# First modulation pieces read by whole rows in 8 KB runs, summed over all four at once; load and compute order of the opening changed

## The reference, cut to what matters

```python
shift, scale, gate = jnp.split(jax.nn.silu(c) @ w_mod[l] + b_mod[l], 3, axis=-1)
shift_c, scale_c, gate_c = jnp.split(jax.nn.silu(c_ctx) @ w_mod[l] + b_mod[l], 3, axis=-1)
hc = rms_norm(xc, norm_w[l]) * (1.0 + scale_c) + shift_c
parts_c = split_in(hc @ w_in[l])
```

## Time and profile before

| | |
|---|---|
| median of 3 runs | 1619.99 us (1619.35 to 1620.15) |
| profiled execution, its own time | 1618.67 us |
| its span, first to last instruction | 1616.9 us |
| TensorE busy | 1520.1 us (94% of the span) |
| VectorE, ScalarE, GpSimd busy | 528.8, 454.2, 324.8 us |
| mean granted TensorE clock | 0.978 of full speed |
| moved by DMA | 233.82 MB, mean 145 GB/s |

### The profile page before, as it was taken

The page is one execution under the profiler, slowest core; times in us unless marked ns, Lnnn a source line. Parts: engine busy times, 40 slices in busy tenths (PEclk is TensorE's granted clock), DMA queues, the critical chain, the costliest instruction groups (busy, mean ns, idle before and its releaser), DMA issues.

```text
span 1616.9 us, 17425 instructions
## 1 busy us (share of the span) xinstructions
PE 1520.1 (94%) x6805; PEld 793.1 (49%) x6805; DVE 528.8 (33%) x1136; ACT 454.2 (28%) x890; POOL 324.8 (20%) x350
## 2 busy tenths in 40 slices
PE   5998989999999989999999999999999599989997
PEld 2676544455676454445675344455455433333332
DVE  1073310655533220565532211122143611212125
ACT  2234322232763232233762120133132110101112
POOL 1010000444000010456000000003522234323310
PEclk9999999999999999999999999999999789999999
DMA  9654114221120212111100131201500679999995
GB/s 348 240 212 179 53 54 154 79 105 52 32 77 1 94 52 77 54 53 52 53 3 1 52 104 62 94 2 52 177 36 14 265 264 401 372 415 391 409 419 231
DMA packets 85129, 233.82 MB, mean 145 GB/s; under 512 B 16824, under 2 KB 24766, under 8 KB 70840
## 3 DMA queue, kind: packets, MB, share of 16 engines
q1 hardware_dynamic: 70002, 204.03, 33.5%
q0 software_dynamic: 13824, 24.98, 4.2%
q10 hardware_dynamic: 1222, 3.70, 0.6%
HBM read 266.42 MB, written 16.80 MB: 175 GB/s over the span
## 4 chain that ended last, share of the span: by engine, by line
PE 89%; ACT 3%; DVE 3%; DMA 3%; issue 2%; POOL 0%; SPq 0%; DVEq 0%; POOLq 0%; ACTq 0%
PE PS L1779 19%; PE PS L2199 11%; PE PS L1947 9%; PE PS L2010 7%; PE PS L2225 5%; PE PS L1859 5%; PE PS L1758 4%; PE PS L2008 3%; PE PS L2103 3%; PE PS L1881 3%; PE PS L1869 3%; PE PS L1821 2%; PE PS L2045 1%; DMA RING<-in_w_mod_dram 1%; PE PS L2072 1%
## 5 line engine op out<-in xcount | busy, mean ns | idle before, releaser
L1779 PE MATMUL PS<-RH,RING 128*128 128x512 f32 (+1 forms) x864 | 315.9, 522 | 2.1 <-DMA RING<-in_w_in_dram 2.1
L1779 PEld LDWEIGHTS PS<-RH,RING 128*128 128x128 f32 x864 | 162.4, 190 | 146.9 <-issue 136.1
L1947 PE MATMUL PS<-RING,RY 128*128 128x512 f32 x320 | 139.4, 593 | 0.0
L2199 PE MATMUL PS<-RING,RM 128*64 128x512 f32 x384 | 116.6, 609 | 8.4 <-issue 5.6
L1277 DVE SCALAR_TENSOR_TENSOR RM<-RM,COL 128x512 f32<-128x512 f32 (+1 forms) x180 | 115.1, 707 | 0.2
L624 POOL TENSOR_SCALAR SMALL<-SMALL 128x1 f32<-128x1 f32 (+1 forms) x32 | 9.3, 290 | 525.8 <-ACT WS L852 266.0
L2010 PE MATMUL PS<-RH,RING 128*128 128x512 f32 x256 | 113.8, 593 | 0.0
L1318 DVE TENSOR_REDUCE SMALL<-PS 128x1 f32<-128x768 f32 (+1 forms) x80 | 68.0, 849 | 136.9 <-PE PS L1859 136.8
L1859 PE MATMUL PS<-RK,RH 96*128 96x256 f32 (+1 forms) x288 | 106.2, 488 | 1.1 <-ACT WS L995 0.7
L1947 PEld LDWEIGHTS PS<-RING,RY 128*128 128x128 f32 x320 | 60.1, 190 | 72.7 <-issue 72.7
L2199 PEld LDWEIGHTS PS<-RING,RM 128*64 128x64 f32 x384 | 37.1, 140 | 83.6 <-issue 80.1
(11 more groups left out here) (356 smaller groups left out, 2289.9 us busy)
## 6 DMA issues: line engine op xcount, KB each, us to landing
RING<-in_w_in_dram SPq DMA_DIRECT2D x18, 2048.0 KB, 8.5
RING<-in_w_mod_dram SPq DMA_DIRECT2D x12, 2048.0 KB, 9.0
RING<-in_w_expert_gate_dram SPq DMA_DIRECT2D x19, 1024.0 KB
RING<-in_w_expert_up_dram SPq DMA_DIRECT2D x19, 1024.0 KB
RING<-in_w_out_dram SPq DMA_DIRECT2D x8, 2048.0 KB, 8.8
RK<-in_w_expert_down_dram SPq DMA_DIRECT2D x8, 1024.0 KB
X<-in_w_expert_down_dram SPq DMA_DIRECT2D x8, 1024.0 KB
WS<-in_w_expert_down_dram SPq DMA_DIRECT2D x8, 1024.0 KB
```

Of the source, the lines that this page charges most:

```text
L1779: last = mm(o[:, 0:T], w[:, k, m * P:(m + 1) * P], HT[:, k, 0:T], start=(k == 0), stop=(k == 7))
L1947: last = mm(PS[:, j % 2, :], YT[:, k, t * P:(t + 1) * P], w[:, k, :], start=(k == 0), stop=(k == 7))
L2199: last = mm(PS[64 * z:64 * z + 64, n % 2, :], XGT[n % 2][:, k, 64 * z:64 * z + 64], free(GU[n % 3][z], [2048, 2], [1, DE], off=DE * k), st ...
```

## The change

The first four modulation pieces are no longer 512 columns of all rows, but 256 rows of the first 2048 columns each: a partition gets two runs of 8 KB in place of eight of 2 KB. TensorE adds all four pieces into one PSUM bank, column quarter z on partitions 32z to 32z+31 (8 matmuls per piece as before), ScalarE copies the bank once, four matmuls turn it into columns, and one VectorE addition and the two steps for `AMOD` (`scale_columns`) follow. The order changes on each engine: ScalarE squares the context rows before it copies the parameter columns; VectorE norms them first; TensorE waits for layer 0's parameter rows ahead of the third piece and transposes the context rows ahead of the fourth. SyncE issues pieces 4 and 5 (`in_low`, `in_feat` 2) ahead of the 16 small loads, and VectorE waits for the head weights only where it first uses them.

```diff
--- before.py
+++ after.py
@@ -420,9 +420,15 @@
         NW = len(plan)
         w_in_cols = {"in_low": (0, U0), "in_gate": (GA0, 512)}
 
+        def early(layer, n):
+
+            return layer == 0 and n < 4
+
         def chunk_view(key):
 
             kind, i, n = key
+            if kind == "mod" and early(i, n):
+                return RING[:, use[key] % 3, :].rearrange("p (k c) -> p k c", k=2)
             c = chunk_cols(key)[1]
             return RING[:, use[key] % 3, 0:8 * c].rearrange("p (k c) -> p k c", k=8)
 
@@ -454,6 +460,8 @@
         def chunk_source(key):
             kind, i, n = key
             c0, c = chunk_cols(key)
+            if kind == "mod" and early(i, n):
+                return a["w_mod"][0][2 * P * n:2 * P * n + 2 * P, 0:2048].rearrange("(k p) c -> p k c", p=P)
             if kind == "mod":
                 w = a["w_mod"][i]
             elif kind.startswith("in_"):
@@ -508,7 +516,7 @@
                 sp.dma_start(WUKV[:, :], a["w_ukv"][layer]).then_inc(s_lw, 16)
                 sp.dma_start(WPW[:, :, :], a["cf_pw_w"][layer].rearrange("(k p) c -> p k c", p=P)).then_inc(s_lw, 16)
 
-            for n in range(4):
+            for n in range(6):
                 load_chunk(n)
             for layer in range(2):
                 for m, name in enumerate(("q_head_norm_w", "k_head_norm_w")):
@@ -517,7 +525,7 @@
             sp.dma_start(OH, a["onehot"]).then_inc(s_oh, 16)
             sp.dma_start(RB[0:32, :], a["rel_bias_2"]).then_inc(s_oh, 16)
             load_rows(sp, R1, ROWS, s_rows[1], 1)
-            for n in range(4, NW):
+            for n in range(6, NW):
                 if plan[n] == ("mod", 0, 4):
                     load_layer_weights(0)
                 if plan[n] == ("in_feat", 0, 0):
@@ -1028,12 +1036,10 @@
                     act.wait_ge(p_gb.sem, p_gb.at(i, c))
                     A(GB[:, 512 * c:512 * c + 512], PS[:, 5 + c, :], ACT.Copy).then_inc(a_gb.sem, 1)
 
-            for n in range(4):
-                mod_rows(0, n, 6 + n % 2)
-                if n == 0:
-                    columns(0)
-                if n == 1:
-                    row_scale(0)
+            row_scale(0)
+            columns(0)
+            act.wait_ge(p_mr, 4)
+            A(MR_EARLY[0], PS[:, 6, :], ACT.Copy).then_inc(a_mr, 4)
             for i in (0, 1, 2, 3):
                 if i in (1, 2):
                     row_scale(i)
@@ -1182,6 +1188,11 @@
                 ins.then_inc(v_ch, 1)
                 v.wait_ge(v_ch, chain[0])
 
+            def scale_columns(layer):
+                link(v.tensor_scalar(AMOD[:, layer, :, :], MOD[:, layer, 8:16, :], 1.0, None, ALU.add))
+                nw = free(COL[:, layer, :], [1, 8], [0, 2], off=ROW["norm_w"])
+                return v.tensor_tensor(AMOD[:, layer, :, :], AMOD[:, layer, :, :], nw, ALU.mult)
+
             def modulation(layer, n, bank):
 
                 done = 6 * layer + n + 1
@@ -1192,9 +1203,7 @@
                 last = v.tensor_tensor(MOD[:, layer, c:c + 4, :], free(PS[:, bank, :], [2, 4], [1, 2]), bm, ALU.add)
                 if n == 3:
                     link(last)
-                    link(v.tensor_scalar(AMOD[:, layer, :, :], MOD[:, layer, 8:16, :], 1.0, None, ALU.add))
-                    nw = free(COL[:, layer, :], [1, 8], [0, 2], off=ROW["norm_w"])
-                    last = v.tensor_tensor(AMOD[:, layer, :, :], AMOD[:, layer, :, :], nw, ALU.mult)
+                    last = scale_columns(layer)
                 last.then_inc(v_mod, 1)
                 v.wait_ge(v_mod, done)
 
@@ -1213,8 +1222,6 @@
             def projections(i):
                 T = nt[i] * P
                 q = Q_RANK if i in FULL else 0
-                if i == 0:
-                    v.wait_ge(s_hw, 16 * 5)
                 for t in range(nt[i]):
                     v.wait_ge(g_ur.sem, g_ur.at(i, t))
                     if q:
@@ -1234,6 +1241,8 @@
                                else CFP[:, c - 10, 15:15 + T])
                         v.tensor_tensor(dst, dst, TMP[:, tmp % 2, 0:T], ALU.mult).then_inc(v_f.sem, 1)
                         tmp += 1
+                    if i == 0 and step_beside(i, j) == 0:
+                        v.wait_ge(s_hw, 16 * 5)
                     if step_beside(i, j) is not None and step_beside(i, j) < units[i]:
                         head_sums(i, step_beside(i, j))
                         head_scale(i, step_beside(i, j))
@@ -1384,10 +1393,13 @@
             v.tensor_reduce(PICK2[:, :], free(IDENT, [1, 2], [32, 4]), AX, ALU.add).then_inc(v_pick, 1)
             v.wait_ge(p_col, 1)
             v.tensor_copy(COLB[:, :], PS[:, 0, 0:NROWB]).then_inc(v_pick, 1)
-            for n in range(4):
-                modulation(0, n, 6 + n % 2)
-                if n == 1:
-                    norm_rows(0)
+            norm_rows(0)
+            v.wait_ge(p_mod, 4)
+            v.wait_ge(a_col, 1)
+            link(v.tensor_tensor(free(MOD[:, 0, :, :].rearrange("p k v -> p (k v)"), [8, 4], [2, 4], [1, 2]), free(PS[:, 7, :], [2, 4], [8, 4], [1, 2]),
+                                 free(COL[:, 0, :], [4, 4], [1, 4], [0, 2], off=ROW["b_mod"]), ALU.add))
+            scale_columns(0).then_inc(v_mod, 4)
+            v.wait_ge(v_mod, 4)
             for k in range(4, 8):
                 v.wait_ge(p_xt.sem, p_xt.at(0, k))
                 v.tensor_scalar(HT[:, k, 0:256], turned(0, k), AMOD[:, 0, k, 1:2], mod_col(0, 0, k), ALU.mult, ALU.add).then_inc(a_ht.sem, 1)
@@ -1961,20 +1973,22 @@
                 pe.wait_ge(v_o.sem, v_o.through(i))
 
             pe.wait_ge(a_sc, 1)
-            mod_rows(0, 0, 6)
-            pe.wait_ge(s_rows[0], 16 * len(ROWS))
-            tr(PS[:, 1, 0:NROW], R0[0:NROW, :], IDENT[0:NROW, 0:NROW]).then_inc(p_col, 1)
-            mod_rows(0, 1, 7)
-            pe.wait_ge(v_pick, 1)
-            mod_columns(0, 0, 6)
-            pe.wait_ge(v_mod, 1)
-            mod_rows(0, 2, 6)
-            mod_columns(0, 1, 7)
-            turn_rows(0)
-            pe.wait_ge(v_mod, 2)
-            mod_rows(0, 3, 7)
-            mod_columns(0, 2, 6)
-            mod_columns(0, 3, 7)
+            for n in range(4):
+                if n == 2:
+                    pe.wait_ge(s_rows[0], 16 * len(ROWS))
+                    tr(PS[:, 1, 0:NROW], R0[0:NROW, :], IDENT[0:NROW, 0:NROW]).then_inc(p_col, 1)
+                if n == 3:
+                    turn_rows(0)
+                w = loaded(("mod", 0, n))
+                for k in range(2):
+                    for z in range(4):
+                        last = mm(PS[32 * z:32 * z + 32, 6, :], SC2[:, 2 * n + k, :], w[:, k, 512 * z:512 * z + 512],
+                                  start=(n == 0 and k == 0), stop=(n == 3 and k == 1))
+                last.then_inc(p_mr, 1)
+            pe.wait_ge(a_mr, 4)
+            for m in range(4):
+                last = mm(PS[:, 7, 8 * m:8 * m + 8], MR_EARLY[0][:, m * P:(m + 1) * P], free(IDENT, [32, 4], [1, 2]), start=True, stop=True)
+            last.then_inc(p_mod, 4)
 
             for i in FULL:
                 if i > 0:
```

## The result

The changed kernel takes 1623.85 us (median of 8 runs, 1623.19 to 1626.23); the kernel before, run beside it, 1620.76 (8 runs). The ratio is 1.0024, 95% interval 1.0014 to 1.0033: 2.3 to 5.3 us slower, 3.9 in the middle (the two medians lie 3.1 apart). The forecast was slower by 7.5 us, about twice as much. The profiled execution took 1623.35 us, its span is 1621.5.

A forecast was written before the change was run, and what follows sets the result against it. TensorE's work from the first projection on bounds the kernel: context landing 33.0 + 14.0 puts that start at 47.0 against 39.59, +7.5 us, so 1619.99 + 7.5 = 1627.5 us; own range 1624 to 1630.5, 8-in-10 range 1618.5 to 1631.

The forecast's parts named there:

- What bounds, and that a shift arrives: TensorE is busy 94% of the span; a shift of the first projection's start (39.59 us) reaches the end undiminished.
- One packet for one packet: ScalarE's and SyncE's DMA queues share engines by packets, not bytes; each packet waits for one 8 KB run, 0.32 us.
- Two engines hold back the context rows: The two DMA engines carrying the 62-row load finish the context rows last, landing at 33.0 us against 19.6.
- The sign that both queues would have equal counts from 5 to 25 us: ScalarE's and SyncE's DMA queues would show equal packet counts between 5 and 25 us.
- the 63 small packets: Packets of sixteen small loads ahead of context on each slow engine: 0.37 us a turn, the last landed about 29.
- From the landing to the start: 14.0: Context landing to first projection: 7.4 us through the transposes, then 6.6 from the fourth piece's matmuls through the hidden rows.
- The start of the chain: Opening: c lands at 12.5, first matmuls near 13.6 against 10.55, no starvation, fourth piece landed near 28.3.
- SyncE's order costs nothing: in_low and in_feat ahead of the small loads: those land by 50, are wanted at 60, so cost nothing.
- Rival one: Opening: delivery does not hold back context, there by about 20; start 35.0 to 37.0, likely -4 us; chance 0.14.
- Rival two: 8 KB run counts as two turns: context 25.3, start 39.3, time 1619.7; break-even a landing at 25.5; chance 0.10.
- Rival three: c so late that SyncE's queue runs empty: context near 27, fourth piece late, about +2 to +4 us; chance 0.06.
- The order of TensorE's waits: Third piece's matmuls are held until the column rows land at 29; the start still follows the context landing at 33.0.

The follow-up runs named there:

- e2: Changed kernel with the 62-row load cut into transfers of 48 and 14 rows; ratio 0.9998 to the kernel before.
- e4: Kernel before with only SyncE's load order changed (pieces 4 and 5 ahead of the small loads) and VectorE's head-weights wait moved; ratio 1.0002.
- e1: Changed kernel with each of the first four pieces fetched by four transfers, runs of 2 KB instead of 8; ratio 0.9979 to the kernel before.
- e5: Changed kernel with each of the first four pieces fetched by two transfers, runs of 4 KB; ratio 0.9976 to the kernel before.
- e7: Changed kernel with the 62-row load issued once more, into unused columns, ahead of the context rows; ratio 1.0025 to the kernel before.
- e3: Changed kernel with the context load issued ahead of the ten small loads; ratio 1.0014 to the kernel before.
- e11: e3 with TensorE's wait for the small rows moved behind the transposes, ahead of the fourth piece; ratio 0.9977 to the kernel before.
- e10: e1 with the 62-row load issued once more ahead of the context rows; ratio 0.9989 to the kernel before.
- e9: e1 run a second time, unchanged; ratio 0.9977 to the kernel before.

## Why the prediction was right, and what it mis-sized

The mechanism was right: the context rows, delayed turn by turn behind 8 KB runs, set the start, and the start set the end. The size was not. Of the forecast +7.5 us some half came, and 1623.85 lies just under the forecast's own range of 1624 to 1630.5. The landing came 3.6 us early and the way from it to the start took 1.0 us more than in the sum.

*What bounds, and that a shift arrives.* Right. Start +4.8, span +4.6. For shifts of 2 us, as in e2 and e4, one profiled start does not tell the time.

*One packet for one packet.* Right, and the reason for the result. e1, e5 and the changed kernel differ in run length (and in the transfers per piece, see e1) and put the first square at 19.2, 22.5 and 29.4. The Trainium skill ("DMA: Bandwidth & Descriptors", section "Queues, rings and completion order") has the engines take turns packet by packet, with 9 to 17 descriptors typically in one; the turns here were single runs of 2 or 8 KB, so the first half agrees and the typical number does not occur.

*Two engines hold back the context rows.* Right: the last 32 of the 256 rows passed from 25 to 29 us, and e2 moved the rows ahead of them by 7 us with the same bytes. The context rows themselves moved by 3 us only: spreading the 62 rows does not bring them back to 20, as their own packets then stand beside 8 KB runs. The sign that both queues would have equal counts from 5 to 25 us did not come (929 against 537): the counts come near each other, 561 against 467 until 18 us, only while most engines have work from both queues.

*The term that was off: the 63 small packets.* In the sum they reach from 7.5 to a landing at 29, 21.5 us: 57 turns at 0.37 us less 1 us for completions, and six short ones. Measured: the constants landed at 7.4, the first six loads at 10.8 (forecast 12.5), the ten others at 25.8 (29), the context rows at 29.4 (33.0). From 7.4 to 25.8 that is 18.4 us, 0.29 a packet. Where only data packets go, from 20 to 24 us, a turn took 0.33 and not 0.37. From 12 to 15 us completions are among them. Of the 27 packets under 2 KB there, at least 4 are SyncE's, as its 108 packets with 0.85 MB hold 104 whole runs; at most 23 on two engines in 3 us are 0.26 us each or more. With 47 data packets at 0.33, the 16 completions are left with some 0.18 each, an estimate: they did not cost a full turn, and the 1 us that the sum took off for them was too little. Why e2's 27 data packets come to 0.26 and not to 0.33 stays open. The error had no chance to show in the sum for the kernel before, where the other queue's run costs 0.084.

*From the landing to the start: 14.0.* Measured 15.0. Squares, roots and norms took 4.5 for 4.1, as GpSimd's step before the second root took 0.60 in place of 0.22 before; the transposes 3.46 for 3.3; the fourth piece's matmuls 2.50 for 2.1. The stretch from 24 to 36 us in the changed kernel (PE, PEld, DVE, ACT, POOL busy, PEclk, DMA share, GB/s):

```profile
24.00:36.00 12.00, 6.61 (x28) 3.08 (x29) 1.51 (x2) 2.45 (x5) 1.98 (x4) 0.50 0.99 369
```

TensorE's granted clock was at the lower level; it had been idle from 18.2 to 25.8. The projection itself then took 13.60 instead of 13.13, and is why the delay is +5.25 behind it. The prediction called 3.64 us for a piece's matmuls the slow clock; its own rows give 1.00 for that stretch, and it is the changed kernel that shows 3.64 beside 0.50, at 26.16.

*The start of the chain.* c at 12.5 and matmuls at 13.6 were forecast, 10.8 and 11.8 measured; the queue did not run empty, as said. The fourth piece at 28.3, measured 27.3.

*SyncE's order costs nothing.* Right by e4.

*The rivals.* Rival one (context not held back) is false for this kernel, but e1 is its world: start 36.7, inside its 35.0 to 37.0. Rival two (an 8 KB run as two turns) is false: 111 against 108. Its break-even, a context landing at 25.5, is supported: e2 landed at 26.4 and is at 0.9998 (0.9989 to 1.0007), though its profiled start is 2 us late. Rival three did not happen in the changed kernel; a gap in the queue such as it describes is how I read e7.

*The order of TensorE's waits.* The prediction noted that the small rows would land at 29 and hold up the third piece, and priced it at nothing because the context rows were later still. That was right for the changed kernel and would have been wrong for its repair: e3 lost 5.5 us to it against e11.

## What to carry to other kernels

When two queues feed the same engines, as here SyncE's and ScalarE's, count packets, not bytes: a load on one queue takes as many turns of the other queue's run length as it has packets on its fullest engine. Before lengthening the runs of a bulk stream, look what small transfers share the engines, put what is needed first ahead in its queue, cut a transfer whose row count has no large divisor up to 16 (62 rows went over two engines), and let the consumer wait for late rows as late as it can. Having removed one late load, look for the next one under it before you run.

## What the runs showed of the hardware that was not expected

- A backlog of small packets can go through in a burst: 83 packets of ScalarE's queue in a microsecond in e7, against 12 in the same window of the changed kernel. That the other queue had run empty is argued. Doubling a load of 62 rows cost 1.2 us there and 3.4 us in e10, where SyncE's queue had 99.2% of the engines from 19 to 23 us.
- A transfer's issue can take 3.36 us instead of 0.40 (e7), and the engine's own work behind the issue waits with it. One more 62-row transfer ahead of it is not enough for that: in e10 the same issue took 0.41.
- From 8 to 26 us the engines moved 386 and 387 GB/s with 2 KB runs (e1, e9), 407 with 4 KB (e5) and 418 with 8 KB. The stretch of the changed kernel:

```profile
8.00:26.00 18.00, 5.75 (x34) 1.38 (x34) 0.20 (x1) 1.32 (x4) 1.24 (x1) 0.87 1.02 418
```
